# Block 2 of a two-block transformer kernel: in2's chunks in another order, and the gated attention placed between weight steps

## The reference

```python
def token_mixer(h, w_in, b_f, lb, g_o, w_out):          # h is the normed input
    z = h @ w_in                                        # 2048 x 7176
    q_a, k_a, v_a, f_a = z[..., 0:1024], z[..., 1024:2048], z[..., 2048:3072], z[..., 3072:3080] + b_f
    y_fox = forgetting_attention(q_a, k_a, v_a, f_a)    # 8 heads of 128, softmax with cumulated log gates
    q_b, f_b, i_b, g_b = (four parts of 1024 columns)
    log_f = log_sigmoid(f_b)                            # the lower bound is 0 at depth 1
    k_b = sigmoid(-f_b)
    o_b = hgrn2_recurrence(q_b, k_b, i_b, log_f)        # 8 heads of 128
    o_b = rms_norm(o_b, g_o) * silu(g_b)
    return concatenate([y_fox, o_b]) @ w_out            # 2048 x 2048
```

## Time and profile before

| | |
|---|---|
| median of 3 runs | 2625.67 us |
| profiled execution | 2625.73 us, its span 2623.9 us |
| mean granted TensorE clock | 0.977 |
| TensorE busy | 2503.5 us (95%) |
| VectorE busy | 1498.3 us (57%) |
| ScalarE busy | 1226.6 us (47%) |
| POOL busy | 70.6 us (3%) |
| HBM over the span | 170 GB/s |

### The profile page before, as it was taken

One profiled execution on the slowest core, in us unless ns is written; L12 is line 12 of the kernel. 1 busy time (PEld: TensorE's weight loads), 2 busy tenths in 40 slices (PEclk: granted clock), 3 DMA queues, 4 the chain that ended last, 5 costly groups with the idle time before them and its releaser, 6 DMA issues. The chain is left out here.

```text
span 2623.9 us, 33048 instructions
## 1 busy us (share of the span) xinstructions
PE 2503.5 (95%) x11851; PEld 2082.0 (79%) x11851; DVE 1498.3 (57%) x1769; ACT 1226.6 (47%) x1530; POOL 70.6 (3%) x98
## 2 busy tenths in 40 slices
PE   7999878999999999999999996999999999999997
PEld 5788646888888888888888886878888888888876
DVE  4655685555454544444644549666666666644465
ACT  4544254444444443444444453445655556544453
POOL 1001300000000000000000002000000000000000
PEclk9999869999999999999999998999999999999999
DMA  7765003666666666555665551456565565565543
GB/s 239 221 184 168 26 1 104 185 190 190 189 190 186 192 185 207 193 191 188 185 183 168 159 156 48 139 152 191 177 191 186 182 187 179 197 204 194 194 165 136
DMA packets 232757, 446.26 MB, mean 170 GB/s; under 512 B 14016, under 2 KB 22932, under 8 KB 232148
## 3 DMA queue, kind: packets, MB, share of 16 engines
q1 hardware_dynamic: 230468, 435.10, 53.7%
q0 software_dynamic: 2192, 9.83, 1.1%
HBM read 442.78 MB, written 2.10 MB: 170 GB/s over the span
## 5 line engine op out<-in xcount | busy, mean ns | idle before, releaser
L1086 DVE TENSOR_TENSOR wlo<-raw,whi 128x1024 fp32r<-128x1024 f32 (+2 forms) x836 | 1005.6, 1209 | 998.3 <-ACT whi L596 997.2
L596 ACT ACTIVATE whi<-raw 128x1024 fp32r<-128x1024 f32 (+2 forms) x836 | 870.7, 1044 | 1175.0 <-PE pg L1829 1138.1
L1827 PE MATMUL pg<-whi,AH 128*128 128x512 f32 (+2 forms) x2240 | 866.6, 387 | 15.4 <-DVE AL L1194 8.7
L1829 PE MATMUL pg<-whi,AL 128*128 128x512 f32 (+2 forms) x2240 | 860.1, 384 | 0.0
L1828 PE MATMUL pg<-wlo,AH 128*128 128x512 f32 (+2 forms) x2240 | 859.7, 384 | 0.0
L1827 PEld LDWEIGHTS pg<-whi,AH 128*128 128x128 f32 x2240 | 421.3, 188 | 99.1 <-DVE AL L1194 9.8
L1829 PEld LDWEIGHTS pg<-whi,AL 128*128 128x128 f32 x2240 | 421.1, 188 | 83.6
L1828 PEld LDWEIGHTS pg<-wlo,AH 128*128 128x128 f32 x2240 | 421.5, 188 | 80.7
L1827 PE MATMUL pg<-whi,FH 128*128 128x512 f32 x704 | 274.4, 390 | 0.0
L1829 PE MATMUL pg<-whi,FL 128*128 128x512 f32 x704 | 274.0, 389 | 0.0
L1828 PE MATMUL pg<-wlo,FH 128*128 128x512 f32 x704 | 273.9, 389 | 0.0
(11 more groups left out here) (391 smaller groups left out, 1482.9 us busy)
## 6 DMA issues: line engine op xcount, KB each, us to landing
raw<-w_up SPq DMA_DIRECT2D x264, 512.0 KB, 3.8
raw<-w_in SPq DMA_DIRECT2D x176, 512.0 KB, 3.7
raw<-w_down SPq DMA_DIRECT2D x176, 512.0 KB, 3.6
raw<-w_gate SPq DMA_DIRECT2D x88, 512.0 KB, 3.6
raw<-w_out SPq DMA_DIRECT2D x64, 512.0 KB, 3.6
raw<-w_ple_gate SPq DMA_DIRECT2D x32, 512.0 KB, 4.0
raw<-w_in SPq DMA_DIRECT2D x16, 288.0 KB, 3.0
raw<-w_in SPq DMA_DIRECT2D x16, 260.0 KB, 3.0
```

Source lines behind the costliest of these rows:

```text
L596: A(whi[:, n % RING, 0:w], raw[:, n % RING, 0:w], ACT.Copy).then_inc(hi_ready, 1)
L1086: V.tensor_tensor(wlo[:, n % RING, 0:w], raw[:, n % RING, 0:w], whi[:, n % RING, 0:w].bitcast(F32), ALU.subtract).then_inc(lo_ready, 1)
L1827: mm(o, xh, wh, start=first and k == 0, stop=False)
L1829: ins = mm(o, xl, wh, start=False, stop=last and k == SK - 1)
```

## The change

in2's columns are computed in another order, so that the forget gates (HF) come first, then the queries of the gated attention (HQ) with fox's gates (F), fox's q and k, the gated attention's values (HI), fox's v, and the output gate (HG) last. All loads of in2 are unrolled on SP. The gated attention's stages become hooks between in2's steps: level l starts at step 46 + 4l. Levels 1 to 7 multiply the full 128 x 128 key tile by only the 64 query columns that lie in second halves. All element work of the levels is on VectorE and ScalarE, none on POOL. Its buffers LG and KB lie in parts of z that are not yet computed. fox's units move to step 93 + 2u in another order. The mixed result is turned in four quarters, two in in2's last chunk and two in out2, and out2's first two chunks are done in halves of k.

```diff
+IN2 = [(O2_HF, CW), (O2_HF + CW, CW), (O2_HQ + CW, CW), (O2_F, 260), (O2_F + 260, 260)]
+IN2 += [(o + i * CW, CW) for o in (0, O2_K, O2_HI, O2_V, O2_HG) for i in range(2)]
+HF_IN, HQ_IN, F_IN, Q_IN, K_IN, HI_IN, V0_IN, V_IN, HG0_IN = 2, 5, 4, 7, 9, 11, 12, 13, 14
+FOX_UNITS = [(0, 0), (0, 1), (1, 0), (1, 1), (0, 2), (0, 3), (1, 2), (1, 3)]
+def at_step(n):
+    return divmod(n, KT // SK)
+def lv_start(l):
+    return 46 + 4 * l
+def fox_start(u):
+    return 93 + 2 * u
...
 POOL
-                for l in range(1, 8):
-                    pool.wait_ge(lv_exp, l + 1)
-                    pool.tensor_tensor(g[:, :, 1, :], g[:, :, 1, :], q[:, :, 1, :], ALU.mult).then_inc(lv_mul_q, 1)
+                pool.wait_ge(step_used, G["down1"]["end"])
+                pool.memset(HS[:], 0.0).then_inc(zeroed, 1)
...
 ScalarE
+            between = {(0, 2): in2(3), (0, 3): norm_final, (0, 6): norm_mix,
+                       (2, 1): hgrn_sig, (2, 3): lambda: link(A(tmp, f, ACT.Abs)),
+                       (2, 5): lambda: link(A(tmp, tmp, ACT.Exp, scale=-1.0)), (2, 7): hgrn_log, (4, 2): hgrn_sums, (5, 2): hgrn_q,
+                       (5, 4): fox_log, (5, 0): lambda: lv_decay(0), (5, 3): lambda: lv_decay(1),
+                       (9, 7): fox_q, (10, 4): fox_sums, (11, 2): ho_squares, (11, 4): ho_root,
+                       (14, 2): lambda: hg_gate(0), (14, 4): mix2(0), (14, 6): mix2(1)}
+            for l in range(8):
+                if 2 <= l + 1 < 8:
+                    between[at_step(lv_start(l) + 2)] = lambda l=l: lv_decay(l + 1)
+                if l < 3:
+                    between[at_step(lv_start(l) + 3)] = lambda l=l: lv_copy(l)
+            between.update({at_step(fox_start(u) + 1): lambda u=u: fox(u) for u in range(10)})
...
 VectorE
+            def lv_times(l):
+                dve.wait_ge(lv_exp, l + 1)
...
+                V.tensor_tensor(g[:, :, :, 0, :], g[:, :, :, 0, :], k[:, :, :, 0, :], ALU.mult)
+                V.tensor_tensor(g[:, :, :, 1, :], g[:, :, :, 1, :], q[:, :, :, 1, :], ALU.mult).then_inc(lv_mul, 1)
+            def lv_take(l):
+                dve.wait_ge(lv_sum, l + 2)
...
+                V.copy_predicated(dst, bc(mask.unsqueeze(1), 16, n, b), src).then_inc(lv_taken, 1)
...
+                       (3, 1): hgrn_min, (3, 4): hgrn_logf, (4, 5): hgrn_k, (4, 7): lambda: lv_differ(0), (5, 1): lambda: lv_differ(1),
+                       (5, 3): fox_abs, (5, 5): lambda: (fox_log(), lv_diagonal()),
+                       (10, 1): fox_k, (11, 2): ho_gain, (11, 3): ho_sums, (11, 6): ho_norm,
+                       (14, 3): lambda: hg_times(0), (14, 4): mix2(0), (14, 6): mix2(1)}
+            for l in range(8):
+                between[at_step(lv_start(l))] = lambda l=l: lv_times(l)
+                if 2 <= l + 1 < 8:
+                    between[at_step(lv_start(l) + 1)] = lambda l=l: lv_differ(l + 1)
+                if l >= 3:
+                    between[at_step(lv_start(l) + 3)] = lambda l=l: lv_take(l)
+            between.update({at_step(fox_start(u)): lambda u=u: fox(u) for u in range(10)})
...
+            between = {2: lambda: hg_times(1), 3: mix2(2), 5: mix2(3)}
...
 TensorE
+            def lv_level(l):
+                pe.wait_ge(lv_mul, l + 1)
...
+                    for t in range(NT):
+                        for h in range(8):
+                            g = LG[l % 2][:, t, h * P:(h + 1) * P]
+                            ins = mm(pt[:, lv_bank(l) + t, h * 64:(h + 1) * 64], g, g.rearrange("p (m a b) -> p m a b", a=2, b=b)[:, :, 1, :],
+                                     start=True, stop=True)
+                ins.then_inc(lv_sum, 1)
...
+            hooks = {(4, 1): hgrn_sums, (4, 4): hgrn_k, (5, 1): hgrn_q, (5, 4): lv_diagonal,
+                     (9, 6): fox_q, (10, 0): fox_k, (10, 2): lambda: fox_sums(0), (10, 3): lambda: fox_sums(4), (11, 1): hgrn_out,
+                     (14, 3): lambda: fox_turn(0), (14, 5): lambda: fox_turn(1)}
+            hooks.update({at_step(lv_start(l) + 1): lambda l=l: lv_level(l) for l in range(8)})
+            hooks.update({at_step(fox_start(u)): lambda u=u: fox(u) for u in range(10)})
...
+            out2(0, 0, 4, 0, ready)
+            out2(1, 0, 4, 4, turn_late)
+            out2(0, 4, 8, 4, ready)
+            out2(1, 4, 8, 8)
+            out2(2, 0, 8, 16)
+            out2(3, 0, 8, 24)
```

More of the change, by code:

```diff
@@ L128, in plan @@
         ("down1", full("w_down", 4), FKT),
-        ("in2", full("w_in_2", 13) + tail("w_in_2", 13 * CW, D_IN2), KT),
+        ("in2", [("w_in_2", c0, w) for c0, w in IN2], KT),
         ("out2", full("w_out_2", 4), KT),
@@ L916, in hgrn_sums @@
                 act.wait_ge(hc_sum, 1)
[L917 to L938, removed]
-                A(EPSC[:, 2:3], EPSC[:, 0:1], ACT.Sqrt)
@@ L996, in norm_mix @@
                 norm(4, H[:, 0, :], D, XN[:, 0, :], None)
-            between = {(0, 2): in2(3), (0, 3): norm_final, (0, 6): norm_mix, (3, 2): fox_q, (7, 1): fox_log, (7, 5): fox_sums,
-                       (11, 1): hgrn_sig, (11, 2): lambda: link(A(tmp, f, ACT.Abs)),
-                       (11, 3): lambda: link(A(tmp, tmp, ACT.Exp, scale=-1.0)), (11, 4): hgrn_log, (12, 2): hgrn_sums}
-            between.update({fox_place(u, 1): lambda u=u: fox(u) for u in range(10)})
+            between = {(0, 2): in2(3), (0, 3): norm_final, (0, 6): norm_mix,
[10 more added lines that the diff above has]
+            between.update({at_step(fox_start(u) + 1): lambda u=u: fox(u) for u in range(10)})
             stream(G["in2"], evac_copy(Z2, G["in2"], SM[:, 4:5]), between, loop=False)
             if upto < 13: return
-            chunks_read(act, G["out2"]["C"])
-            hgrn()
-            if upto < 14: return
-            stream(G["out2"], evac_squares(G["out2"], 0), {(0, 3): mix2(2), (0, 4): mix2(3)})
+            between = {1: lambda: hg_gate(1), 3: mix2(2), 5: mix2(3)}
+            evac = evac_squares(G["out2"], 0)
+            for i in range(32):
+                between.get(i, no)()
+                split(G["out2"]["N"] + RING + i)
+                if i in OUT2_ENDS:
+                    evac(OUT2_ENDS[i], 0, G["out2"]["N"] + i + 1)
             post_root(5)
@@ new lines, in hgrn_sums, with hgrn_k @@
+                for t in range(NT):
+                    for h in range(8):
+                        c0 = O2_HF + h * P
+                        ins = mm(head_place(t, h), Z2[:, t, c0:c0 + P], tri64, start=True, stop=True)
+                ins.then_inc(hc_sum, 1)
+            def hgrn_k():
+                pe.wait_ge(hc_out, 1)
+                for t in range(NT):
+                    for h in range(8):
+                        ins = tr(head_place(t, h), KB[:, t, h * P:(h + 1) * P], ident)
+                ins.then_inc(hk_turned, 1)
@@ new lines, in hgrn_q, with lv_diagonal @@
+            def hgrn_q():
+                chunks_read(pe, G["in2"]["C"] + HQ_IN)
+                pe.wait_ge(hk_out, 1)
+                for t in range(NT):
+                    for h in range(8):
+                        ins = tr(head_place(t, h), Z2[:, t, O2_HQ + h * P:O2_HQ + (h + 1) * P], ident)
+                ins.then_inc(hq_turned, 1)
+            def lv_diagonal():
+                pe.wait_ge(hq_out, 1)
+                for t in range(NT):
+                    for h in range(8):
+                        ins = mm(head_place(t, h), HKT[:, t, h * P:(h + 1) * P], HQ[:, t, h * P:(h + 1) * P], start=True, stop=True)
+                ins.then_inc(lv_sum, 1)
@@ new lines, in hgrn_out @@
+            def hgrn_out():
+                chunks_read(pe, G["in2"]["C"] + HI_IN)
+                pe.wait_ge(fc_out, 1)
+                pe.wait_ge(lv_taken, 6)
+                for t in range(NT):
+                    for h in range(8):
+                        v = [Z2[:, i, O2_HI + h * P:O2_HI + (h + 1) * P] for i in range(NT)]
+                        if t:
+                            mm(head_place(t, h), HX[:, h, :], v[0], start=True, stop=False)
+                        ins = mm(head_place(t, h), HS[:, t, h * P:(h + 1) * P], v[t], start=not t, stop=True)
```

422 lines of the change are left out of this document (207 added, 215 removed).

## The result

| | before | after |
|---|---|---|
| median of 4 runs | 2624.40 us (2622.75 to 2627.27) | 2640.48 us (2638.68 to 2647.63) |
| ratio, 95% interval | | 1.0065 [1.0044, 1.0086] |
| profiled execution, span | 2625.73, 2623.9 us | 2647.63, 2645.8 us |
| mean granted clock | 0.977 | 0.972 |

The change makes the kernel 0.65% slower. 2624.0 us was forecast, and 2640.5 lies above the range of 2608 to 2636. The medians differ by 16.1 us. From in2's first weight matmul to out2's last (1238.90 to 1744.37 us before, 1240.14 to 1767.31 us after) the traces differ by 21.7 us, so the loss lies there.

What follows compares the result with a forecast made beforehand. TensorE, busy 95% of the span, was taken as the bound. Products of 43.8 us plus waits of 28.8 less 82.6 removed gave -10.0; with 8.4 for the clock, -1.6 on 2625.7: 2624 us, range 2608 to 2636.

Steps and rivals of the forecast that it cites:

- What can be removed, 82.6 us: Serial gated attention between in2 and out2, 80.6 us without weight steps, plus 2.0 us of TensorE waits inside in2.
- what comes in, 43.8: TensorE time the change adds to the weight stream: 384 records of turns, levels and products at 0.114 us, 43.8 us.
- 64 columns cost as many as 128: In levels 1 to 7, halving the moving columns saves TensorE nothing: 0.114 us a record, bounds 0.057 and 0.23.
- Rival 3: In levels 1 to 7, 64 columns cost half: 12.8 us less, 2611 us; chance 0.09.
- The waits, 28.8 us: New TensorE pauses in the stream: levels 1 to 7 15.4, turned q 3.9, level 0 3.1, other places 6.4 us.
- turned q: Transposes of the gated attention's queries at step 41: TensorE waits 3.9 us for VectorE to copy chunk 4.
- rival 4: In two fine levels, strided 64-column reads or the masked copy cost more: +7.3 us, 2631 us; chance 0.10.
- Rival 1: VectorE is less closely tied to TensorE, so level waits and their clock losses vanish: 2605 us; chance 0.14.
- out2's order at 0: In out2, the new order costs 0 us, since preparations come 2 to 3 steps before use; 1.3 us if not.
- The clock, 8.4 us: Low clock after new pauses: 4.0 us for a third of seven level pauses, 4.4 for two long ones; bounds 0, 18.7.
- Rival 2: TensorE's clock falls after every pause, 1.7 us each at levels and 3.4 at two long ones: 2634 us; chance 0.17.
- -1.6: Forecast change of the whole kernel in us against the profiled execution of 2625.7 us; chance 0.45.

Runs made afterwards that it cites:

- the spaced kernel: The changed kernel with the plan moved one to four steps later wherever a wait stood, and the square-root table loaded early; 2588.32 us, ratio 0.9853 to before.

## Why the prediction was wrong

Point by point, with the balance against 2647.63 us:

- *What can be removed, 82.6 us, and what comes in, 43.8.* Right in their difference, to about 1 us, by the spaced kernel; no run shows the two apart.
- *64 columns cost as many as 128 (0.114 us a record).* Right: 224 records take 25.9 us in the spaced kernel and 26.0 us at 128 columns. Rival 3, the half price, is out. The half price is also what the issue gap of the Trainium skill gives ("TensorE: Matmul & The Clock Gate", Back-to-back issue gap); these two rows, 0.116 us a record at either width, don't agree with it for fp32 products with 128 x 128 weights.
- *The waits, 28.8 us.* 30.3. Levels 16.4 for 15.4, turned q 4.0 for 3.9, level 0 2.9 for 3.1, `fox_sums` 2.0 for 2.1, `fox_q` 2.3 for 1.0. The last, and the level wait of 3.3 us before level 7, come from the masked copy (the first by its releaser, L1663; the second by the order on VectorE, which no run isolates): it takes 1.28 us down to blocks of 4 and 2.4 to 2.5 us for blocks of 2 and 1, of which I had written that above 1.4 us I should be wrong on VectorE. So the second cause that rival 4 names is there, at 2.4 us instead of its 7.3; the first, dearer reads of 64 columns in the fine levels, is not. Rival 1 is out.
- *out2's order at 0.* Right for TensorE's waits; undoing the halves of k brings one of 0.8 us. Missed is the table load at its end: the edit moved the Silu past the square root's table, which I did not follow on ScalarE; 1.4 us in the trace.
- *The clock, 8.4 us.* **This is the step that failed.** It cost 28 us: 24 behind the level pauses where I had 4.0 + 2.2, 2.6 at the turned q for 2.2, and 1.7 behind `fox_q` for nothing. I took a third of the seven level pauses at 1.7 us each, by pauses in the serial part of before, and set the upper bound at 18.7 by one stretch of 3.4 us per pause. Six of the seven had one, so the count was wrong; and they lasted 6.8 or 10.2 us and nearly doubled the time of the narrow products (6.71 us for 3.79) and of the weight matmuls behind them, so the price was wrong. The longer stretches were in the trace before: of its five in the serial part two last 6.8 us, one of them in the earlier trace rows, the other from 1582.7 us, and I priced with the shorter. Rival 2, which had the count, had the same price and so came out at 2634 us. What I had not asked is what TensorE runs directly behind the pause. Level 0 (128 columns, 2.9 us) had none.

The sum: -1.6 + 1.5 (waits) + 19.6 (clock) + 1.4 (table) = +20.9 us, of 21.9 measured on the slowest of the four executions. The medians are 16.1 us apart; how much low clock the shorter executions had is not shown beyond their mean granted clock, 0.973 to 0.975 for 0.972.

What the runs show of the cause: the low clock comes with the pauses, and the narrow products directly behind them make it come oftener and last longer. Without the level pauses (levels a step later, or pauses filled) the levels run at full clock, but for one stretch of 6.8 us behind a pause of 1.3 us. With the pauses and wide products, or with a weight step between, 13.7 and 17 us of low clock are left in in2 instead of 58, each stretch behind a level pause 3.4 us long. A pause does not need narrow products to bring a fall: three of the eight brought one with weight matmuls behind them, two with wide products, and the pause of 4.0 us at the turned q brought 6.8 us in every kernel that has it, with 128 columns behind it.

What stays open is why a pause is followed by the low clock in one place and not in the next equal one: level 4 of the changed kernel has the pause of level 1 (2.0 us) and the same products, and stays at 1.00. The wide products and the weight step also move everything behind them in time, and no run separates that from what stands behind the pause. The Trainium skill names frequent short idle times between groups of matmuls as what makes the clock swing ("TensorE: Matmul & The Clock Gate", A second HAM failure mode: psum-queue depth-cycling); the runs agree in that the low clock goes with the pauses (58 us with them, 6.8 with them filled).

## What to carry over

A wait put into a dense stream of matmuls costs its own length and then what the clock takes, and in this kernel that depended on the work behind it. Moving the products one step later, so that there is no wait, gave most (2601.1 us); wide products behind the pause gave some (2625.6). Before halving the columns of an fp32 product with full weights, see whether it saves anything; here it saved nothing and made the pauses dear. When a plan is moved, follow the engine's last function too, since a table load moves with it.

## What the runs showed of the hardware

- A pause of 2.0 us before 32 records of 64 columns was followed by 1.2 GHz for up to 10.2 us; one of 2.9 us before 128 columns by none. Nearly the same pauses gave 58 us (narrow behind them), 17 us (narrow a step later) and 13.7 us (wide) at 1.2 GHz in in2.
- TensorE kept busy with products that nobody reads, where it would have paused, makes the kernel faster: 2624.1 against 2640.5 us.
- 224 fp32 records with 128 x 128 weights take 25.9 us at 64 moving columns and 26.0 us at 128.
- The masked copy of 128x1024 takes 1.3 us, and 2.4 to 2.5 us where the runs under the mask are 1 or 2 elements long (levels 6 and 7).
